# One PSUM group, one copy and one subtraction for the transposed weights of the first two query blocks

## The chip, the cores and the metric

The kernel runs on one core of a Trainium2 chip. The metric is the device time of one execution, in microseconds (us). The core has five engines with instruction streams of their own, which meet only in semaphores: TensorE (PE, with its weight loads shown as PEld), VectorE (DVE), ScalarE (ACT), GpSimd (POOL) and SyncE (SP).

## What is computed

The program is a whole transformer step for one sequence of 512 tokens and 1024 channels: a feed-forward layer, a mixer, a second feed-forward layer, and then a hybrid layer. The part that matters here is the attention of the hybrid layer, with 16 heads of 64 channels, in float32:

```python
def stick_breaking_attention(q, k, v):
    S = q.shape[2]
    outs = []
    for i in range(S // BLOCK_Q):
        q0, q1 = i * BLOCK_Q, (i + 1) * BLOCK_Q
        qb, kb, vb = q[:, :, q0:q1], k[:, :, :q1], v[:, :, :q1]
        z = jnp.einsum('bhqd,bhkd->bhqk', qb, kb).astype(jnp.float32) * SB_SCALE
        mask = jnp.arange(q1)[None, :] < jnp.arange(q0, q1)[:, None]
        log_1m_beta = jnp.where(mask, -jax.nn.softplus(z), 0.0)
        suffix = lax.cumsum(log_1m_beta, axis=3, reverse=True) - log_1m_beta
        w = jnp.where(mask, jnp.exp(jax.nn.log_sigmoid(z) + suffix), 0.0)
        outs.append(jnp.einsum('bhqk,bhkd->bhqd', w.astype(vb.dtype), vb))
    return jnp.concatenate(outs, axis=2)
```

Query block i (128 queries) sees the keys of blocks 0 to i, so its weights are a matrix of 128 by (i+1)*128. It has to be transposed, block by block, before it can be multiplied with the values.

## The kernel before

The attention works in 8 rounds (PAIRS), each for one pair of heads h = 0 and 1. Round 0 is written out, rounds 1 to 6 are one hardware loop, round 7 is written out again. Products are made from float32 split into a high and a low part, three matmuls for one (`three`, L2307 to L2309).

A round on TensorE is two weight slots of the large input projection (`in_slot`), 8 steps of 6 matmuls each, with 512 columns to a matmul. Between these steps stand the small pieces of the attention. Where each stands is written by hand in three tables, one for each engine: ATT_PE, ATT_ACT and ATT_DVE. A key from 0 to 15 is the step of the round, and its list is what runs ahead of that step's matmuls. So each engine's order is fixed, and only semaphores join them. The pieces are:

- ("Q", h, i): the scores of query block i, three matmuls on TensorE (L2754 to L2756); ScalarE makes two sigmoids of them (L1204, L1205), VectorE a scan and a product (L2076, L2080), which leaves the weights in the tile Wt and counts w_done.
- ("T", h, i): the transposes of query block i. TensorE turns i+1 blocks of 128 columns into PSUM bank 6 (L2772) and counts t_mm. ScalarE copies them to wTh, the high part (L1224), and counts thi_done. VectorE subtracts that copy from the bank into wTl, the low part (L2100), and counts tlo_done. All groups share bank 6, so a group on TensorE waits until the subtraction of the group ahead of it is done (`tlo_done`, L2770). The first of a round waits for the values' low part instead (`vlo_done`).
- ("PV", h): the weights by the values, eight matmuls (L2781, L2782). It needs all four groups of its head.
- ("hi", n, half) and ("lo", n, half): high and low part of half a weight slot (L1255 on ScalarE, L2132 on VectorE).
- ("k low",), ("q low",), ("q own",), ("k other",), ("sum", 0), ("V",), ("v2",): keys, queries, sums and values for this round and the next.

I write T(h,i) for the group of head h and query block i. The eight groups stand at steps 4, 5, 7, 8 for h = 0 and at steps 10, 12, 13, 15 for h = 1. Behind T(1,1) on TensorE come the six matmuls of step 12, then T(1,2). The wait of a group reads:

```python
pe.wait_ge(w_done, r * 8 + (idx + 1))
if idx == 0:
    pe.wait_ge(vlo_done, r + 1)
else:
    pe.wait_ge(tlo_done, r * 8 + idx)
for b in range(i + 1):
    last = nc.tensor.transpose(ps[:, 6, b * P:(b + 1) * P], wt_of(i)[:, b * P:(b + 1) * P], ident[:])
last.then_inc(t_mm, 1)
```

Of the kernel before, what the change touches and what calls it, by code (L numbers as in the profile page):

```python
# [16 lines left out]
fp32 = mybir.dt.float32  # L17
f32r = mybir.dt.float32r
bf16 = mybir.dt.bfloat16
ALU = mybir.AluOpType  # L20
ACT = mybir.ActivationFunctionType
AX = mybir.AxisListType

P = 128
T = 512
# [72 lines left out]
for n, (_, _, during) in enumerate(MIXER):  # L98
    for k in sorted(during):
        for step in during[k]:  # L100
            if n >= 2 and step[0] in ("S", "cols", "vt", "mm", "hy"):
                at = 8 * n + k + 3 if n > 3 else 8 * n + min(k + 1, 7)
# [12 lines left out]
MIX_READ = {entry[:2]: n + 1 for n, entry in enumerate(MIXER)}  # L115


ATT_PE = {0: [("Q", 0, 0), ("Q", 0, 1), ("PV", 1), ("V",)], 1: [("Q", 0, 2)], 2: [("Q", 0, 3)], 4: [("T", 0, 0), ("Q", 1, 0)],
          5: [("T", 0, 1)], 7: [("Q", 1, 1), ("T", 0, 2), ("Q", 1, 2)], 8: [("T", 0, 3)], 9: [("Q", 1, 3)],
          10: [("PV", 0), ("T", 1, 0)], 12: [("T", 1, 1)], 13: [("T", 1, 2)], 15: [("T", 1, 3)]}  # L120
ATT_ACT = {0: [("v2",), ("Q", 0, 0), ("sum", 1), ("Q", 0, 1), ("hi", 0, 0), ("V",)], 1: [("Q", 0, 2)], 2: [("Q", 0, 3), ("gah",)],
# [3 lines left out]
ATT_DVE = {0: [("Q", 0, 0), ("sum", 1), ("gate",), ("Q", 0, 1), ("lo", 0, 0), ("V",)], 1: [("Q", 0, 2)],  # L125
# [3 lines left out]
ATT_LATE = ("PV", 1), ("sum", 1), ("gate",), ("gah",), ("gal",)  # L129

# [24 lines left out]
def program(nc, a, out):  # L155
    with ExitStack() as ctx:
# [21 lines left out]
        ident = sb("ident", [P, P])  # L178
# [251 lines left out]

        def wt_of(i):
            return Wt[:, i * (i + 1) // 2 * P:(i + 1) * (i + 2) // 2 * P]

        HALF = slice(0, DK), slice(DK, 2 * DK)

# [340 lines left out]
        def _(act):  # L776
# [420 lines left out]
            def att_step(step, r):  # L1197
                kind, h = step[0], step[1] if len(step) > 1 else 0
                if kind == "Q":
                    i = step[2]  # L1200
                    idx, n = 4 * h + i, (i + 1) * P
                    act.wait_ge(q_mm, r * 8 + (idx + 1))
                    act.wait_ge(w_done, r * 8 + max(idx - 1, 0))
                    nc.scalar.activation(g1[:, idx % 2, 0:n], ps[:, 4 + idx % 2, 0:n], ACT.Sigmoid, scale=-1.0)  # L1204
                    nc.scalar.activation(be[:, idx % 2, 0:n], ps[:, 4 + idx % 2, 0:n], ACT.Sigmoid).then_inc(sig_done, 1)  # L1205
                elif kind == "V":
                    act.wait_ge(v_mm, r + 1)
                    act.wait_ge(pv_mm, r * 2)
                    bank = ps[:, 6, :].rearrange("p (b d) -> p b d", d=P)
                    for e in range(2):  # L1210
                        last = nc.scalar.activation(vph[:, e, :, HALF[e]], bank[:, :, HALF[e]], ACT.Copy)
                    last.then_inc(vhi_done, 1)
                    for e in range(2):
                        last = nc.scalar.activation(vp[:, e, :, HALF[e]], bank[:, :, HALF[e]], ACT.Copy)
                    last.then_inc(vp_done, 1)
                elif kind == "sum":
                    act.wait_ge(pv_mm, r * 2 + 1 if h == 0 else r * 2)
                    nc.scalar.activation(pvl[HALF[h], :], ps[HALF[1 - h], 7, :], ACT.Copy).then_inc(pv_low, 1)
                elif kind == "T":
                    i = step[2]  # L1220
                    idx = 4 * h + i
                    act.wait_ge(t_mm, r * 8 + (idx + 1))
                    act.wait_ge(pv_mm, r * 2 + h)
                    nc.scalar.activation(wTh[:, 0:i + 1, i * P:(i + 1) * P],  # L1224
                                         ps[:, 6, 0:(i + 1) * P].rearrange("p (b t) -> p b t", t=P), ACT.Copy).then_inc(thi_done, 1)
                elif kind == "gah":
                    act.wait_ge(ga_done, r)
                    nc.scalar.activation(gah[:, r - 1:r, :] if isinstance(r, int) else gah[:, bass.ds(act.snap(r - 1), 1), :],
                                         ga[:].unsqueeze(1), ACT.Copy).then_inc(gah_done, 1)
                elif kind == "hi":  # L1230
                    if isinstance(r, int) and r == PAIRS - 1:
                        hi_half(S_POOL + h + 1, step[2])
                    else:
                        hi_half(S_ATT + h + 3, step[2], r)
                elif kind == "v2":
                    act.wait_ge(slot_used, r * 2 + (S_ATT + 2))
                    nc.scalar.activation(v2[:], ps[:, 2, :], ACT.Copy).then_inc(ve_done, 1)
                elif kind == "sz":
                    act.wait_ge(slot_used, r * 2 + (S_ATT + 2))
                    act.wait_ge(zs_done, r)  # L1240
                    nc.scalar.activation(sz[:], ps[:, 3, :], ACT.Sigmoid).then_inc(sz_done, 1)
                elif kind == "k own":
                    read_k(r + 1)
                elif kind == "q own":
                    read_q(r + 1)
                elif kind == "k other":
                    read_k_other(r + 1)
# [163 lines left out]
        def _(dve):  # L1411
# [656 lines left out]
            def att_step(step, r):  # L2068
                kind, h = step[0], step[1] if len(step) > 1 else 0
                if kind == "Q":  # L2070

                    i = step[2]
# [22 lines left out]
                elif kind == "T":  # L2095
                    i = step[2]
                    idx = 4 * h + i
                    dve.wait_ge(thi_done, r * 8 + (idx + 1))
                    place = (slice(None), slice(0, i + 1), slice(i * P, (i + 1) * P))
                    nc.vector.tensor_tensor(wTl[place], ps[:, 6, 0:(i + 1) * P].rearrange("p (b t) -> p b t", t=P),  # L2100
                                            wTh[place].bitcast(fp32), ALU.subtract).then_inc(tlo_done, 1)
                elif kind == "gate":
                    dve.wait_ge(pv_sum, r * 2)
                    dve.wait_ge(zs_done, r)
# [199 lines left out]
        def _(pe):  # L2304
# [438 lines left out]
            def att_step(step, r):  # L2743
# [19 lines left out]
                elif kind == "T":  # L2763
                    i = step[2]
                    idx = 4 * h + i
                    pe.wait_ge(w_done, r * 8 + (idx + 1))
                    if idx == 0:
                        pe.wait_ge(vlo_done, r + 1)
                    else:
                        pe.wait_ge(tlo_done, r * 8 + idx)  # L2770
                    for b in range(i + 1):
                        last = nc.tensor.transpose(ps[:, 6, b * P:(b + 1) * P], wt_of(i)[:, b * P:(b + 1) * P], ident[:])  # L2772
                    last.then_inc(t_mm, 1)
                elif kind == "PV":

                    pe.wait_ge(tlo_done, r * 8 + 4 if h == 0 else r * 8)
# [176 lines left out]
```

## Time and profile before

| | before |
|---|---|
| median of 3 runs | 1530.57 us (1530.33 to 1530.58) |
| the profiled execution | 1530.44 us |
| span of its trace | 1528.8 us |
| TensorE busy | 1514.4 us (99%), 8932 matmuls |
| VectorE busy | 1014.7 us (66%) |
| ScalarE busy | 714.4 us (47%) |
| mean granted TensorE clock | 0.999 of full speed |

Durations come from the profiled execution. A row of the trace gives a start and a duration. TensorE's matmuls overlap: one of 512 columns is shown for 0.39 us, but the next one starts 0.23 us after it. So what a piece costs TensorE is read from the distance of the starts, and its duration only tells when its result is there. The start of a weight load (PEld) shows when a waiting matmul was let go, since the load comes first.

### The profile page before, as it was taken

To read this page: it belongs to the slowest core of one execution; us is meant where nothing else is said; L and a number is where in the kernel's file an instruction comes from. 1 tells how busy PE (TensorE), PEld (TensorE's weight loads), DVE (VectorE), ACT (ScalarE), POOL (GpSimd) and SP (SyncE) were. 2 spreads that over 40 slices of the span, in tenths; PEclk is the share of its full clock that TensorE was granted. 3 is DMA by queue.
4 is the path that set the end of the run, shared out by engine and by line. 5 is a ranking of instruction groups with operands and counts; after the bars stand their busy time and mean duration, and the time that the engine had idled before them with its cause. 6 is when DMAs were issued, how large, how long until landed. Compare 5 with 4: busy or idle time off the path is not lost.

```text
span 1528.8 us, 23058 instructions
## 1 busy us (share of the span) xinstructions
PE 1514.4 (99%) x8932; PEld 1334.6 (87%) x8932; DVE 1014.7 (66%) x1206; ACT 714.4 (47%) x1045; POOL 54.1 (4%) x101
## 2 busy tenths in 40 slices
PE   8999999999999999999999999999999999999998
PEld 7999998889888889899998888788888888888887
DVE  5888884237766838888885766688888775423243
ACT  6545543236566337545443224566666633312134
POOL 1000000002100002000000001000000000000001
PEclk9999999999999999999999999999999999999999
DMA  5233323322331231333326752222222222332321
GB/s 196 83 111 110 97 70 136 110 82 84 99 98 56 83 111 56 111 111 99 97 80 233 247 179 61 68 66 55 82 71 66 71 95 83 110 111 82 110 83 55
DMA packets 134909, 153.23 MB, mean 100 GB/s; under 512 B 3600, under 2 KB 123532, under 8 KB 134844
## 3 DMA queue, kind: packets, MB, share of 16 engines
q1 hardware_dynamic: 131584, 137.38, 28.5%
q0 software_dynamic: 3024, 14.88, 2.9%
q8 instruction: 46, 0.75, 0.2%
q14 instruction: 19, 0.16, 0.0%
q10 hardware_dynamic: 236, 0.06, 0.0%
HBM read 150.08 MB, written 2.23 MB: 100 GB/s over the span
## 4 chain that ended last, share of the span: by engine, by line
PE 96%; DVE 2%; ACT 1%; issue 0%; DMA 0%; DVEq 0%; ACTq 0%
PE ps L2307 21%; PE ps L2309 21%; PE ps L2308 21%; PE ps L2506 16%; PE ps L2511 8%; PE ps L2772 1%; PE ps L2670 1%; PE ps L2782 1%; PE ps L2755 1%; PE ps L2781 1%; PE ps L2754 1%; PE ps L2388 0%; PE ps L2737 0%; PE ps L2448 0%; DVE wl L1417 0%
## 5 line engine op out<-in xcount | busy, mean ns | idle before, releaser
L2307 PE MATMUL ps<-ah,wh 128*128 128x512 f32 (+1 forms) x1344 | 515.5, 384 | 3.1 <-DVE al L1471 1.2
L2309 PE MATMUL ps<-ah,wl 128*128 128x512 f32 (+1 forms) x1344 | 503.8, 375 | 0.0
L2308 PE MATMUL ps<-al,wh 128*128 128x512 f32 (+1 forms) x1344 | 503.0, 374 | 0.0
L2307 PEld LDWEIGHTS ps<-ah,wh 128*128 128x128 f32 x1344 | 253.8, 189 | 48.8 <-issue 2.3
L2309 PEld LDWEIGHTS ps<-ah,wl 128*128 128x128 f32 x1344 | 252.9, 188 | 45.9
L2308 PEld LDWEIGHTS ps<-al,wh 128*128 128x128 f32 x1344 | 253.5, 189 | 41.1
L1417 DVE TENSOR_TENSOR wl<-raw,wh 128x2048 fp32r<-128x2048 f32 x52 | 119.1, 2291 | 164.7 <-ACT wh L790 164.5
L790 ACT ACTIVATE wh<-raw 128x2048 fp32r<-128x2048 f32 x53 | 101.3, 1911 | 196.9 <-PE ps L2309 193.2
L2506 PE MATMUL ps<-al,wh 128*128 128x256 f32 x576 | 141.3, 283 | 0.0
L2506 PE MATMUL ps<-ah,wh 128*128 128x256 f32 x576 | 141.3, 283 | 0.0
L2506 PEld LDWEIGHTS ps<-al,wh 128*128 128x128 f32 x576 | 110.6, 192 | 0.1
L2506 PEld LDWEIGHTS ps<-ah,wh 128*128 128x128 f32 x576 | 110.6, 192 | 0.1
L2506 PE MATMUL ps<-sh,wh 128*128 128x256 f32 x432 | 106.0, 283 | 0.0
L2506 PE MATMUL ps<-sl,wh 128*128 128x256 f32 x432 | 106.0, 283 | 0.0
L2253 DVE TENSOR_TENSOR wl<-raw,wh 128x2048 fp32r<-128x2048 f32 x16 | 36.7, 2292 | 91.8 <-ACT wh L1345 91.8
L1345 ACT ACTIVATE wh<-raw 128x2048 fp32r<-128x2048 f32 x16 | 30.7, 1917 | 127.3 <-PE ps L2309 127.3
L2506 PEld LDWEIGHTS ps<-sh,wh 128*128 128x128 f32 x432 | 82.9, 192 | 0.0
L2506 PEld LDWEIGHTS ps<-sl,wh 128*128 128x128 f32 x432 | 82.9, 192 | 0.0
L2511 PE MATMUL ps<-ah,wl 128*128 128x256 f32 x576 | 80.9, 283 | 0.0
L2511 PEld LDWEIGHTS ps<-ah,wl 128*128 128x128 f32 x576 | 74.3, 192 | 0.0
L1649 DVE TENSOR_TENSOR wl<-raw,wh 128x1024 fp32r<-128x1024 f32 x54 | 66.0, 1222 | 11.5 <-ACT wh L961 11.5
L981 ACT ACTIVATE hid<-gate 128x512 f32 (+1 forms) x36 | 22.8, 633 | 100.1 <-DVE gate L1702 100.1
(397 smaller groups left out, 2404.3 us busy)
## 6 DMA issues: line engine op xcount, KB each, us to landing
raw<-in_w_ffn_in SPq DMA_DIRECT2D x74, 512.0 KB, 3.6
raw<-in_w_ffn_out SPq DMA_DIRECT2D x22, 1024.0 KB, 5.0
raw<-in_w_in SPq DMA_DIRECT2D x36, 512.0 KB, 4.8
raw<-in_w_in SPq DMA_DIRECT2D x14, 1024.0 KB, 5.6
ada_raw<-in_w_ada POOLq DMA_DIRECT2D x8, 1536.0 KB, 7.3
raw<-in_w_mix_in SPq DMA_DIRECT2D x10, 1024.0 KB, 5.3
raw<-in_w_ffn_in SPq DMA_DIRECT2D x7, 1024.0 KB, 5.2
raw<-in_w_mix_out SPq DMA_DIRECT2D x4, 1024.0 KB, 4.9
```

The lines of the kernel that those rows point to most:

```text
L790: nc.scalar.activation(wh[n % 2][:], raw[n % 2][:], ACT.Copy).then_inc(hi_done, 2 if n + 1 in AHEAD else 1)
L981: nc.scalar.activation(hid[:, bass.ds(i * 4 + 2 * (PLAIN[f] + par), 2), COLS[h]], (gate1, gate2)[h][:], ACT.Silu).then_inc(gate_silu, 1)
L1345: nc.scalar.activation(wh[n % 2][:], raw[n % 2][:], ACT.Copy).then_inc(hi_done, 1)
L1417: nc.vector.tensor_tensor(wl[n % 2][:], raw[n % 2][:], wh[n % 2][:].bitcast(fp32), ALU.subtract).then_inc(lo_done, 2 if n + 1 in AHEAD else 1)
L1649: nc.vector.tensor_tensor(ring_of(wl, f, k), weight_of(f, PRODUCTS[k]), ring_of(wh, f, k).bitcast(fp32), ALU.subtract).then_inc(p_lo, 1)
L2253: nc.vector.tensor_tensor(wl[n % 2][:], raw[n % 2][:], wh[n % 2][:].bitcast(fp32), ALU.subtract).then_inc(lo_done, 1)
L2307: nc.tensor.matmul(bank, w[0], m[0], start=start, stop=False, skip_group_check=shared)
L2308: nc.tensor.matmul(bank, w[0], m[1], start=False, stop=False, skip_group_check=shared)
L2309: return nc.tensor.matmul(bank, w[1], m[0], start=False, stop=stop, skip_group_check=shared)
L2506: nc.tensor.matmul(ps[:, bank, COLS[nb]], ring_of(wh, f, k)[:, kk, nb * P:(nb + 1) * P], (high, low)[part][:, kk, :], start=name in OPENS ...
L2511: last = nc.tensor.matmul(ps[:, bank, COLS[nb]], ring_of(wl, f, k)[:, kk, nb * P:(nb + 1) * P], high[:, kk, :], start=False, stop=kk == KD ...
L2670: last = nc.tensor.matmul(ps[:, 6 + w, at:at + DV + 1], E[:, u % 2, b, t * P:(t + 1) * P], vS[:, h, b, :], start=j == 0, stop=j == len(see ...
```

## The change

T(h,0) and T(h,1) become one group, at the place of T(h,1). TensorE's entries ("T", h, 0) go out of the three tables. The entry ("T", h, 1) now makes three transposes in bank 6: block (query 0, key 0) in the first quarter, (query 1, key 0) in the second and (query 1, key 1) in the fourth. The third quarter keeps whatever was there. One ScalarE copy and one VectorE subtraction take the whole bank as 2 times 256 columns; what lands from the third quarter in wTh and wTl is never read, since the value matmuls of key block 1 start at query block 1. The counters step by 2 at once, so that all later counts stay as they were. The merged group waits for the values' low part with h = 0, and for the group ahead of it with h = 1.

```diff
-ATT_PE = {0: [("Q", 0, 0), ("Q", 0, 1), ("PV", 1), ("V",)], 1: [("Q", 0, 2)], 2: [("Q", 0, 3)], 4: [("T", 0, 0), ("Q", 1, 0)],
+ATT_PE = {0: [("Q", 0, 0), ("Q", 0, 1), ("PV", 1), ("V",)], 1: [("Q", 0, 2)], 2: [("Q", 0, 3)], 4: [("Q", 1, 0)],
...
-          10: [("PV", 0), ("T", 1, 0)], 12: [("T", 1, 1)], 13: [("T", 1, 2)], 15: [("T", 1, 3)]}
+          10: [("PV", 0)], 12: [("T", 1, 1)], 13: [("T", 1, 2)], 15: [("T", 1, 3)]}
...
+        def turned_blocks(i):
+
+            return [(0, 0, 0), (1, 0, 1), (1, 1, 3)] if i == 1 else [(i, b, b) for b in range(i + 1)]
+
+        def turned_place(i):
+
+            first, n = (0, 2 * P) if i == 1 else (i * P, P)
+            return (slice(None), slice(0, i + 1), slice(first, first + n)), ps[:, 6, 0:(i + 1) * n].rearrange("p (b t) -> p b t", t=n)
+
...
-                    nc.scalar.activation(wTh[:, 0:i + 1, i * P:(i + 1) * P],
-                                         ps[:, 6, 0:(i + 1) * P].rearrange("p (b t) -> p b t", t=P), ACT.Copy).then_inc(thi_done, 1)
+                    place, turned = turned_place(i)
+                    nc.scalar.activation(wTh[place], turned, ACT.Copy).then_inc(thi_done, 2 if i == 1 else 1)
...
-                    place = (slice(None), slice(0, i + 1), slice(i * P, (i + 1) * P))
-                    nc.vector.tensor_tensor(wTl[place], ps[:, 6, 0:(i + 1) * P].rearrange("p (b t) -> p b t", t=P),
-                                            wTh[place].bitcast(fp32), ALU.subtract).then_inc(tlo_done, 1)
+                    place, turned = turned_place(i)
+                    nc.vector.tensor_tensor(wTl[place], turned, wTh[place].bitcast(fp32), ALU.subtract).then_inc(tlo_done, 2 if i == 1 else 1)
...
-                    if idx == 0:
+                    if idx == 1:
                         pe.wait_ge(vlo_done, r + 1)
                     else:
-                        pe.wait_ge(tlo_done, r * 8 + idx)
-                    for b in range(i + 1):
-                        last = nc.tensor.transpose(ps[:, 6, b * P:(b + 1) * P], wt_of(i)[:, b * P:(b + 1) * P], ident[:])
-                    last.then_inc(t_mm, 1)
+                        pe.wait_ge(tlo_done, r * 8 + (idx if i > 1 else idx - 1))
+                    for q, b, at in turned_blocks(i):
+                        last = nc.tensor.transpose(ps[:, 6, at * P:(at + 1) * P], wt_of(q)[:, b * P:(b + 1) * P], ident[:])
+                    last.then_inc(t_mm, 2 if i == 1 else 1)
```

The first place: TensorE in the loop, from the last value matmul of PV(0) to the matmuls of step 10. Before:

```order
L2782 MATMUL ps<-wTl,vph 128x256
L2781 MATMUL ps<-wTh,vp 128x128
L2782 MATMUL ps<-wTl,vph 128x128
L2772 MATMUL ps<-ident,Wt 128x128 [waits tlo_done,w_done]
L2307 MATMUL ps<-ah,wh 128x512
L2308 MATMUL ps<-al,wh 128x512
```

and after:

```order
L2790 MATMUL ps<-wTl,vph 128x256
L2789 MATMUL ps<-wTh,vp 128x128
L2790 MATMUL ps<-wTl,vph 128x128
L2315 MATMUL ps<-ah,wh 128x512
L2316 MATMUL ps<-al,wh 128x512
```

The lone transpose of T(1,0) is gone from here, and the projection's matmul follows the value matmul at once.

The second place: TensorE in the loop, from T(1,1) over step 12 to T(1,2). Before:

```order
L2772 MATMUL ps<-ident,Wt 128x128 [waits tlo_done,w_done]
L2772 MATMUL ps<-ident,Wt 128x128
L2307 MATMUL ps<-ah,wh 128x512
L2308 MATMUL ps<-al,wh 128x512
L2309 MATMUL ps<-ah,wl 128x512
L2307 MATMUL ps<-ah,wh 128x512
L2308 MATMUL ps<-al,wh 128x512
L2309 MATMUL ps<-ah,wl 128x512
L2766 REGISTER_ALU
L2772 MATMUL ps<-ident,Wt 128x128 [waits tlo_done,w_done]
```

and after:

```order
L2780 MATMUL ps<-ident,Wt 128x128 [waits tlo_done,w_done]
L2780 MATMUL ps<-ident,Wt 128x128 x2
L2315 MATMUL ps<-ah,wh 128x512
L2316 MATMUL ps<-al,wh 128x512
L2317 MATMUL ps<-ah,wl 128x512
L2315 MATMUL ps<-ah,wh 128x512
L2316 MATMUL ps<-al,wh 128x512
L2317 MATMUL ps<-ah,wl 128x512
L2774 REGISTER_ALU
L2780 MATMUL ps<-ident,Wt 128x128 [waits tlo_done,w_done]
```

The group has one transpose more, and the same six matmuls stand between it and the next group.

The third place: ScalarE in the loop, from the first half of the weight slot's high part to the sum behind T(1,1). Before:

```order
L1255 ACTIVATE wh<-raw 128x1024 [waits slot_used]
L1223 REGISTER_ALU [waits t_mm]
L1224 ACTIVATE wTh<-ps 128x128 [waits pv_mm]
L1255 ACTIVATE wh<-raw 128x1024
L1224 ACTIVATE wTh<-ps 128x2x128 [waits pv_mm,t_mm]
L1267 ACTIVATE q<-ps 64x512 [waits q_mm]
L1267 ACTIVATE q<-ps 64x512
L1218 ACTIVATE acc<-ps 64x512 [waits pv_mm]
```

and after:

```order
L1264 ACTIVATE wh<-raw 128x1024 [waits slot_used]
L1264 ACTIVATE wh<-raw 128x1024
L1232 REGISTER_ALU [waits t_mm]
L1234 ACTIVATE wTh<-ps 128x2x256 [waits pv_mm]
L1276 ACTIVATE q<-ps 64x512 [waits q_mm]
L1276 ACTIVATE q<-ps 64x512
L1227 ACTIVATE acc<-ps 64x512 [waits pv_mm]
```

The copy is of 512 columns in place of 256, and the wait for TensorE (t_mm) has moved from the copy itself to a register instruction ahead of it. In rounds 0 and 7 the copy itself waits, before and after.

## Rows read from the trace of the kernel before

**Rows 1.** Page, head: busy time, share of the span, instructions.
```profile
span 1528.8 us, 23058 instructions
PE 1514.4 (99%) x8932; PEld 1334.6 (87%) x8932; DVE 1014.7 (66%) x1206; ACT 714.4 (47%) x1045; POOL 54.1 (4%) x101
PEclk9999999999999999999999999999999999999999
```

**Rows 2.** Waits, 960 to 1260 us: who waited for whom, total, times, longest.
```profile
ACT wTh L1224 <- PE ps L2772: 65.6, 50, 3.0
DVE wTl L2100 <- ACT wTh L1224: 35.9, 42, 1.6
...
PEld ps L2772 <- issue: 0.4, 1, 0.4
```

**Rows 3.** Lines by form, attention: group, count, busy us, mean ns, idle before.
```profile
L2772 PE MATMUL ps<-ident,Wt 128*128 128x128 f32 x160 | 28.2, 274 | 0.0
...
L2100 DVE TENSOR_TENSOR wTl<-ps,wTh 128x512 fp32r<-128x512 f32 x16 | 11.1, 692 | 8.9 <-ACT wTh L1224 8.9
L1224 ACT ACTIVATE wTh<-ps 128x512 fp32r<-128x512 f32 x16 | 9.6, 600 | 16.1 <-PE ps L2772 16.1
...
L2100 DVE TENSOR_TENSOR wTl<-ps,wTh 128x256 fp32r<-128x256 f32 x16 | 6.7, 421 | 9.5 <-ACT wTh L1224 9.5
L1224 ACT ACTIVATE wTh<-ps 128x256 fp32r<-128x256 f32 x16 | 6.2, 385 | 13.4 <-PE ps L2772 13.4
```

**Rows 4.** Timeline: start, duration, engine; TensorE at T(0,0) and Q(1,0), round 0.
```profile
985.57 0.27 PE L2772 MATMUL ps<-ident,Wt 128*128 128x128 f32 x1
985.59 0.30 PE L2754 MATMUL ps<-k,q 128*128 128x128 f32 x1
...
985.89 0.48 PE L2307 MATMUL ps<-ah,wh 128*128 128x512 f32 x1
```

**Rows 5.** Timeline, TensorE: Q(0,0) of the next round, with no transpose ahead.
```profile
1007.24 0.22 PE L2754 MATMUL ps<-k,q 128*128 128x128 f32 x1
...
1007.46 0.36 PE L2754 MATMUL ps<-k,q 128*128 128x256 f32 x1
```

**Rows 6.** Timeline, TensorE: the last of PV(0), and T(1,0).
```profile
997.72 0.28 PE L2782 MATMUL ps<-wTl,vph 128*128 128x128 f32 x1
...
997.83 0.30 PE L2772 MATMUL ps<-ident,Wt 128*128 128x128 f32 x1
...
998.20 0.39 PE L2308 MATMUL ps<-al,wh 128*128 128x512 f32 x1
```

**Rows 7.** Timeline, round 0: T(1,1), its copy, its subtraction, T(1,2).
```profile
1000.72 0.39 PE L2772 MATMUL ps<-ident,Wt 128*128 128x128 f32 x2
...
1000.86 0.48 PE L2307 MATMUL ps<-ah,wh 128*128 128x512 f32 x1
...
1001.14 0.39 ACT L1224 ACTIVATE wTh<-ps 128x256 fp32r<-128x256 f32 x1 [1.28 <-PE ps L2772]
...
1001.56 0.42 DVE L2100 TENSOR_TENSOR wTl<-ps,wTh 128x256 fp32r<-128x256 f32 x1 [1.19 <-ACT wTh L1224]
...
1002.10 0.48 PEld L2772 LDWEIGHTS ps<-ident,Wt 128*128 128x128 f32 x3
1002.33 0.49 PE L2772 MATMUL ps<-ident,Wt 128*128 128x128 f32 x3
...
1002.57 0.48 PE L2307 MATMUL ps<-ah,wh 128*128 128x512 f32 x1
```

**Rows 8.** Timeline, VectorE at T(1,2), and TensorE's load for T(1,3).
```profile
1003.90 0.54 DVE L2100 TENSOR_TENSOR wTl<-ps,wTh 128x384 fp32r<-128x384 f32 x1
...
1005.19 0.58 PEld L2772 LDWEIGHTS ps<-ident,Wt 128*128 128x128 f32 x4
```

**Rows 9.** Timeline: a late load let go by VectorE, ahead of attention.
```profile
960.19 0.75 DVE L1471 SCALAR_TENSOR_TENSOR al<-tt,mod,ah 128x512 fp32r<-128x512 f32 x1
...
960.99 0.19 PEld L2307 LDWEIGHTS ps<-ah,wh 128*128 128x128 f32 x1 [0.23 <-DVE al L1471]
961.02 0.47 PE L2307 MATMUL ps<-ah,wh 128*128 128x512 f32 x1
```

**Rows 10.** Timeline, round 7: a late load of a transpose group, T(0,3).
```profile
1207.21 0.42 PEld L2772 LDWEIGHTS ps<-ident,Wt 128*128 128x128 f32 x4 [0.37 <-issue]
1207.24 0.63 PE L2772 MATMUL ps<-ident,Wt 128*128 128x128 f32 x4
```

**Rows 11.** Timeline, feed-forward: ScalarE let go by TensorE, twice.
```profile
99.24 1.12 PE L2511 MATMUL ps<-ah,wl 128*128 128x256 f32 x8
...
100.48 1.06 ACT L961 ACTIVATE wh<-sq 128x1024 fp32r<-128x1024 f32 x1 [1.21 <-PE ps L2511]
...
102.12 1.12 PE L2511 MATMUL ps<-ah,wl 128*128 128x256 f32 x8
...
103.28 0.60 ACT L977 ACTIVATE up<-ps 128x512 f32<-128x512 f32 x1 [0.79 <-PE ps L2511]
```

8 rows, old and new, of tables (ATT_ACT, ATT_DVE) are left out of this document.

## The prediction

> **What bounds the kernel now.** I read the head of the page first. TensorE is busy for 99% of the span at a clock granted at its full level, 2.4 GHz, all along, while VectorE stands at 66% and ScalarE at 47% [rows 1]. So only two things can move the time: the distance from one TensorE start to the next, and a wait that TensorE does not have today. The waits of the attention come next. ScalarE waits for the transposes (65.6 us in 50 waits) and VectorE for the copies (35.9 us in 42), but of TensorE's own transpose groups one alone is late, by 0.4 us in all [rows 2]. The time that ScalarE and VectorE save is thus worth nothing by itself. What counts is the transposes' places in TensorE's queue, and how long the chain of transposes, copy and subtraction is, because the next group waits for its end (one bank for all). I looked for the spot where that chain is tightest, which is between T(1,1) and T(1,2).
>
> **What ScalarE and VectorE save.** The merged copy is 600 ns, the merged subtraction 692 ns; the two-block ones are 385 and 421 ns [rows 3]. One copy and one subtraction in each head go. Nobody on TensorE waits for either engine here, so I cost this at nothing. The cover is TensorE's own work; were it gone, this would be a gain of some tenths of a us in a round.
>
> A rule speaks for the change here: the Trainium skill, VectorE: DVE Perf Modes, section "The TRN2 errata", says that each instruction pays a fixed latency and advises tiles of 512 elements or more. Twice the columns take 1.56 times as long on ScalarE (600 over 385) and 1.64 times on VectorE, so the trace agrees. It makes a throughput gain on engines that have time to spare, and adds nothing to the sum.
>
> **TensorE's queue, head 0.** T(0,0) and Q(1,0) together take 985.89 - 985.57 = 0.32 us from start to start [rows 4]. Q without a transpose ahead of it takes 1007.46 - 1007.24 = 0.22 us [rows 5]. So 0.10 us goes at step 4. The merged group has three transposes for two. Two take 1000.86 - 1000.72 = 0.14 us of the queue and three take 1002.57 - 1002.33 = 0.24 us [rows 7], so 0.10 us comes back at step 5. The sum is nothing.
>
> **TensorE's queue, head 1.** From the last value matmul over T(1,0) to the second matmul of step 10 it is 998.20 - 997.72 = 0.48 us [rows 6]. Without the transpose it should be 0.11 us (the distance from the value matmul to its successor, in the same rows) and 0.23 us for a matmul of 512 columns, 0.34 us in all. The trace has no value matmul followed by a projection matmul, so this is bounded: from 0.48 (nothing goes) to 0.34, and I take 0.34, since both matmuls are of the same kind. That is -0.14, and the third transpose at T(1,1) is +0.10: -0.04 us in a round, and 0.3 us in 8 rounds.
>
> **The chain behind T(0,1).** T(0,2) is two steps away, past ten other matmuls or more, and VectorE has the first subtraction of the round less ahead of it. The chain grows by 0.6 us (worked out next) against over 1 us of room, so I expect no wait there.
>
> **The chain behind T(1,1).** Here only six matmuls stand between. In round 0 the group starts at 1000.72, the copy at 1001.14, the subtraction at 1001.56 and ends at 1001.98; TensorE's load for T(1,2) is at 1002.10 [rows 7]. From the end of a VectorE instruction to the load that it releases takes 960.99 - 960.94 = 0.05 us [rows 9]. So the room today is 0.12 - 0.05 = 0.07 us. The change lengthens the chain in three places: the group ends 0.10 us later (the spans of three and two transposes, 0.49 and 0.39 [rows 7]), the copy takes 0.215 us more and the subtraction 0.271 us more [rows 3]. That is 0.59 us. TensorE itself comes 0.10 us later. The load is therefore late by 0.59 - 0.10 - 0.07 = 0.42 us.
>
> TensorE doesn't lose all of that, since a load normally starts ahead of its matmul: 1002.33 - 1002.10 = 0.23 us [rows 7]. A late one starts 0.03 us ahead [rows 9, 10]. So 0.20 us of the lateness is absorbed, and 0.22 us is lost. A group with a late load then takes a little longer in the queue, some 0.02 us by an estimate from the spans, 0.63 against 0.60 for four transposes. I take **0.24 us** for a round.
>
> **The register wait.** In the loop the copy's wait for TensorE now stands on a register instruction ahead of it, and ScalarE has nothing else to do by then. The trace has such a case: ScalarE starts L961 at 100.48, 0.12 us after TensorE's end (99.24 + 1.12); L977, which waits itself, starts 0.04 us after the end at 103.24 [rows 11]. So the chain is 0.08 us longer in the six rounds of the loop. Before, this register wait belonged to T(1,0)'s copy, which ScalarE reached long after the transpose was done. The bounds are 0 and 0.08 us; I take 0.08, since the two forms in the rows are those of the order. A loop round then loses 0.32 us.
>
> **Behind that wait.** Queued behind T(1,2) on TensorE are all later matmuls of the round, and every one shifts. Who is late next? T(1,3) waits for T(1,2)'s subtraction, which ends at 1004.44 with the load at 1005.19 [rows 8]: 0.75 us of room. VectorE comes to it up to 0.6 us later, TensorE 0.3 us later, so about 0.4 us of room stays. The last subtraction of the round follows T(1,3) with both engines idle ahead of it, so PV(1) keeps its distance. The half slots of `hi` and `lo` run earlier than before, since T(0,0) and T(1,0) no longer stand ahead of them on ScalarE and VectorE.
>
> **The sum.** Rounds 0 and 7: 2 x (0.24 - 0.04) = 0.40 us. Rounds 1 to 6: 6 x (0.32 - 0.04) = 1.68 us. Together +2.1 us. The profiled execution took 1530.44 us, 0.13 us under the median; on the median of 1530.57 that is **1532.7 us**, 0.14% slower, within what a measurement of this kernel can hardly tell from no change (0.2%, or 3.1 us).
>
> The Trainium skill states this very effect: Perfetto Trace Analysis, section "Optimizing Scalar/DVE Operations", says that where these engines aren't saturated but cause bubbles on others, breaking instructions up may let work complete sooner. The change is the reverse of that. By this rule the chain decides, as in my sum; by the rule on fixed latency nothing would be lost, which is the first rival. That TensorE's load for T(1,2) comes only 0.12 us after the subtraction's end today [rows 7] agrees with the rule of breaking up; a wait there is shown by no row of before.
>
> **Rivals.**
>
> *No wait appears.* If the load is let go earlier than I work out, only the queue's gain stays: 8 x -0.04 = -0.3 us, 1530.3 us. The point from which it decides is a chain 0.42 us shorter in rounds 0 and 7. Against it: each term is the length of a shape that the trace has 16 times. 12%.
>
> *The wait, and the lone transposes free nothing.* The matmul behind a transpose group has a distance of about 0.32 us to its successor instead of 0.23, and so has the one behind a Q piece. If TensorE pays that after PV(0) too, and Q(1,0) alone still takes 0.32 us, then the 0.10 and 0.14 us do not go. That is 0.24 us a round, 1.9 us in all: 1532.7 + 1.9 = 1534.6 us, slower by 0.27%. It decides from 0.12 us a round on. For it: no row has a value matmul ahead of a projection matmul. Against it: rows 5 have the Q piece alone at 0.22 us. 18%, with what a wait at T(1,3) could add.
>
> *Faster.* For over 3.1 us a round would have to gain 0.4 us, where the two removed groups hold 0.24 us in all. It needs a cost of a group that the starts don't show. 3%.
>
> *The change doesn't do what it says.* The order of the instructions shows one copy and one subtraction in place of two on each engine, and 160 transposes as before, so I give this no chance of its own.
>
> **How the numbers follow.** The forecast has 67%, the rivals 12, 18 and 3%. In its own range the register wait may be worth nothing (-0.5 us), and the wait may be 0.1 us longer or shorter in each round (0.8 us either way): 1531.4 to 1533.5 us. The range for 8 in 10 takes in the upper bound of the queue's term at PV(0) (+1.1 us: 1533.8) and reaches some way to both neighbours: 1530.9 to 1534.2 us. Slower by over 0.2% (from 1533.63 us on) has 19%, faster by over 0.2% 3%, and within it 78%.
>
> **What would show it.** In the changed kernel's waits, TensorE's load for the transposes has 8 waits on the VectorE subtraction. Counted from the end of the load ahead (0.04 us ahead of the normal start), they are of about 0.46 us in rounds 0 and 7 and 0.54 us in the loop. T(1,1)'s copy starts 0.53 us after its group in rounds 0 and 7 and about 0.61 us after it in the loop. Step 10's first matmul follows PV(0) by 0.11 us and its successor follows it by 0.23 us. Q(1,0) takes 0.22 us. Were there no wait at T(1,2), or one at T(0,2), T(1,3) or PV too, the prediction would be wrong in its mechanism; were the distances around the removed groups unchanged, in its size.

## The result, and the profile after

| | before | changed |
|---|---|---|
| median | 1530.57 us (9 runs, 1530.33 to 1530.78) | 1534.60 us (9 runs, 1534.44 to 1534.83) |
| span of the trace | 1528.8 us | 1532.8 us |

The change makes the kernel slower by 4.0 us, a ratio of 1.0026 (95% interval 1.0017 to 1.0036). The forecast was 1532.7 us with 1534.2 as the upper end. The sign and the place were right. The size was not: half of the loss was missing.

The head of the changed kernel's page answers to [rows 1]. The busy times differ by 1 us at most, and 16 instructions are gone on VectorE and on ScalarE, two for each round:

```profile
span 1532.8 us, 23016 instructions
PE 1515.4 (99%) x8932; PEld 1334.4 (87%) x8932; DVE 1015.5 (66%) x1190; ACT 714.1 (47%) x1029; POOL 54.1 (4%) x101
```

Busy times don't show where 4 us went. The waits do. Here are those of the changed kernel from 960 to 1260 us (who waited for whom, total, times, longest), beside [rows 2]:

```profile
PEld ps L2780 <- issue: 6.0, 9, 0.7
...
PE ps L2780 <- DVE wTl L2109: 2.4, 8, 0.3
```

One late load of a transpose group has become nine. Eight of them are new, and TensorE itself sat idle in all eight for the VectorE subtraction. Before, it did not once.

This is T(1,1) to T(1,2) in round 0 of the changed kernel, in order of time, beside [rows 7]:

```profile
1000.61 0.49 PE L2780 MATMUL ps<-ident,Wt 128*128 128x128 f32 x3
...
1000.86 0.47 PE L2315 MATMUL ps<-ah,wh 128*128 128x512 f32 x1
...
1001.19 0.60 ACT L1234 ACTIVATE wTh<-ps 128x512 fp32r<-128x512 f32 x1 [1.65 <-issue]
...
1001.89 0.69 DVE L2109 TENSOR_TENSOR wTl<-ps,wTh 128x512 fp32r<-128x512 f32 x1 [2.04 <-ACT wTh L1234]
...
1002.10 0.40 PE L2317 MATMUL ps<-ah,wl 128*128 128x512 f32 x1
...
1002.70 0.31 PEld L2780 LDWEIGHTS ps<-ident,Wt 128*128 128x128 f32 x3 [0.64 <-issue]
1002.73 0.52 PE L2780 MATMUL ps<-ident,Wt 128*128 128x128 f32 x3 [0.24 <-DVE wTl L2109]
...
1003.00 0.48 PE L2315 MATMUL ps<-ah,wh 128*128 128x512 f32 x1
```

T(1,2) starts 0.63 us after the matmul ahead of it, where the normal distance is 0.23 us. That is 0.40 us lost. The group then takes 1003.00 - 1002.73 = 0.27 us of the queue, 0.02 to 0.03 us more than one that isn't late. In the loop the copy comes later still. This is round 1:

```profile
1031.72 0.49 PE L2780 MATMUL ps<-ident,Wt 128*128 128x128 f32 x3
1032.38 0.60 ACT L1234 ACTIVATE wTh<-ps 128x512 fp32r<-128x512 f32 x1 [1.74 <-PE ps L2780]
...
1033.08 0.69 DVE L2109 TENSOR_TENSOR wTl<-ps,wTh 128x512 fp32r<-128x512 f32 x1 [1.83 <-ACT wTh L1234]
1033.20 0.40 PE L2317 MATMUL ps<-ah,wl 128*128 128x512 f32 x1
...
1033.89 0.31 PEld L2780 LDWEIGHTS ps<-ident,Wt 128*128 128x128 f32 x3 [0.73 <-issue]
1033.92 0.52 PE L2780 MATMUL ps<-ident,Wt 128*128 128x128 f32 x3 [0.32 <-DVE wTl L2109]
```

The distance is 0.72 us here, so 0.49 us are lost. The copy starts 0.66 us after its group, against 1001.19 - 1000.61 = 0.58 us in round 0. This 0.08 us is what the prediction gave the wait on the register instruction.

The queue behind PV(0), beside [rows 6]:

```profile
997.69 0.27 PE L2790 MATMUL ps<-wTl,vph 128*128 128x128 f32 x1
997.80 0.44 PE L2315 MATMUL ps<-ah,wh 128*128 128x512 f32 x1
998.08 0.39 PE L2316 MATMUL ps<-al,wh 128*128 128x512 f32 x1
```

From the last value matmul to the second matmul of step 10 it is 0.39 us, between the 0.34 of the forecast and the 0.48 of before.

The whole loss then adds up from the trace. A round of the kind of 0 and 7 loses 0.40 (late start) + 0.02 (longer group) + 0.01 (queue: -0.09 at T(1,0), +0.10 for the third transpose) = 0.43 us, a round of the loop 0.52 us. 2 x 0.43 + 6 x 0.52 = 4.0 us, which is the difference of the spans.

### The profile page after: what moved, and what is told of

It is laid out like the page before. It is cut to its first block, busy times and chain, and to the rows that moved or that the text cites. A ratio compares the mean times of both kernels' runs of the same rounds, so it can differ in the third digit from the quotient of the medians.

```text
span 1532.8 us, 23016 instructions
## 1 busy us (share of the span) xinstructions
PE 1515.4 (99%) x8932; PEld 1334.4 (87%) x8932; DVE 1015.5 (66%) x1190; ACT 714.1 (47%) x1029; POOL 54.1 (4%) x101
## 4 chain that ended last, share of the span: by engine, by line
PE 95%; DVE 2%; ACT 1%; issue 1%; DMA 0%; DVEq 0%; ACTq 0%
PE ps L2315 21%; PE ps L2317 21%; PE ps L2316 21%; PE ps L2514 16%; PE ps L2519 8%; PE ps L2780 1%; PE ps L2678 1%; PE ps L2790 1%; PE ps L2763 1%; PE ps L2789 1%; PE ps L2762 1%; PE ps L2396 0%; PE ps L2745 0%; DVE wTl L2109 0%; PE ps L2456 0%
```

## Experiments

Each run was timed in several rounds against the kernel before on the same chip, whose median lay between 1530.45 and 1530.55 us.

### Which head, and is it the room

The first question is whether the wait at T(1,2) is all of the loss. Two kernels make the change at one head alone. Their edit is in the condition of the merged group, and in the tables, where the entries of the other head come back:

```diff
-            return [(0, 0, 0), (1, 0, 1), (1, 1, 3)] if i == 1 else [(i, b, b) for b in range(i + 1)]
+            return [(0, 0, 0), (1, 0, 1), (1, 1, 3)] if (h, i) == (0, 1) else [(i, b, b) for b in range(i + 1)]
```

**Head 0 alone (h0).**

> The change at head 0 alone: T(0,0) and T(0,1) merged, T(1,0) and T(1,1) as before. By my steps T(0,2) has over 1 us of room, no wait appears, and TensorE's queue comes out even (0.11 us less at Q(1,0), 0.10 us more at T(0,1)): 1530.4 to 1530.7 us. If a merged group costs something that is not the wait, the time shows half of the whole loss, 1532.4 us.

Measured: 1530.84 us against 1530.55 (ratio 1.0002, 0.9992 to 1.0011). This is T(0,1) to T(0,2) in round 0:

```profile
987.50 0.49 PE L2780 MATMUL ps<-ident,Wt 128*128 128x128 f32 x3
988.08 0.60 ACT L1234 ACTIVATE wTh<-ps 128x512 fp32r<-128x512 f32 x1 [1.37 <-issue]
988.78 0.69 DVE L2109 TENSOR_TENSOR wTl<-ps,wTh 128x512 fp32r<-128x512 f32 x1 [1.28 <-ACT wTh L1234]
990.83 0.32 PEld L2780 LDWEIGHTS ps<-ident,Wt 128*128 128x128 f32 x3
```

The subtraction ends at 989.47, 1.36 us ahead of the load. The same longer chain stands here, and costs nothing that the interval can tell from zero. The time is still 0.1 us above the expected range: a round of the loop takes 30.65 us against 30.61 before. No wait at T(0,2) goes with it, and where these 0.04 us a round come from is open.

**Head 1 alone (h1).**

> The change at head 1 alone: T(1,0) and T(1,1) merged, T(0,0) and T(0,1) as before. The wait at T(1,2) is all of the loss: 8 waits of 0.40 to 0.49 us at the start of T(1,2) against the normal distance, 0.02 us of a longer group and 0.01 us in the queue, 1534.4 us. If the loss is shared by both heads, 1532.4 us.

Measured: 1534.58 us (1.0027, 1.0016 to 1.0037). In its waits TensorE sits idle for the subtraction 8 times, 2.4 us in all, as in the changed kernel. All of the loss is at head 1.

**T(1,1) one step earlier (earlier).**

```diff
-          10: [("PV", 0)], 12: [("T", 1, 1)], 13: [("T", 1, 2)], 15: [("T", 1, 3)]}
+          10: [("PV", 0)], 11: [("T", 1, 1)], 13: [("T", 1, 2)], 15: [("T", 1, 3)]}
```

> The changed kernel with T(1,1) one step earlier in TensorE's table (step 11 in place of 12), so that twelve matmuls stand between it and T(1,2) in place of six. ScalarE's and VectorE's orders, shapes, steps of two and wait orders stay. The room grows by six matmuls, 1.4 us, against a wait of some 0.7 us: no wait at T(1,2), and what stays is the queue alone, +0.01 us a round by the trace of the changed kernel: 1530.4 to 1530.8 us. T(1,1) stands one step behind PV(0) now, and ScalarE finishes its half slot 0.4 us ahead of it. If merging costs anything beside the wait, the time stays above 1531 us.

Measured: 1530.70 us (1.0001, 0.9991 to 1.0011). With twelve matmuls in between, the load of T(1,2) comes when TensorE gets to it:

```profile
999.35 0.49 PE L2780 MATMUL ps<-ident,Wt 128*128 128x128 f32 x3
999.93 0.60 ACT L1234 ACTIVATE wTh<-ps 128x512 fp32r<-128x512 f32 x1 [0.28 <-issue]
1000.63 0.69 DVE L2109 TENSOR_TENSOR wTl<-ps,wTh 128x512 fp32r<-128x512 f32 x1 [0.67 <-ACT wTh L1234]
1002.21 0.48 PEld L2780 LDWEIGHTS ps<-ident,Wt 128*128 128x128 f32 x3
1002.44 0.49 PE L2780 MATMUL ps<-ident,Wt 128*128 128x128 f32 x3
```

The copy is 0.58 us and the subtraction 1.28 us behind the group, as in the changed kernel: the chain is as slow as it was, and one table entry makes 3.9 us of it vanish. So the loss is the room at that one spot.

### How much of it is the length of the chain

**The kernel before with a wide copy at T(1,1) (wide).** On ScalarE:

```diff
-                    nc.scalar.activation(wTh[:, 0:i + 1, i * P:(i + 1) * P],
-                                         ps[:, 6, 0:(i + 1) * P].rearrange("p (b t) -> p b t", t=P), ACT.Copy).then_inc(thi_done, 1)
+                    n = 4 if (h, i) == (1, 1) else i + 1
+                    nc.scalar.activation(wTh[:, 0:n, i * P:(i + 1) * P],
+                                         ps[:, 6, 0:n * P].rearrange("p (b t) -> p b t", t=P), ACT.Copy).then_inc(thi_done, 1)
```

and the same n in VectorE's subtraction.

> The kernel before, all eight groups of a round as they were, but at T(1,1) the copy and the subtraction take the whole bank (512 columns) in place of 256; the other two quarters land where nobody reads. Nothing else differs: no merged group, no step of two, the register wait stays at T(1,0)'s copy. It measures the length of the chain alone. By my working the chain is 0.215 + 0.271 = 0.49 us longer against 0.07 us of room, late by 0.42 us; 0.20 us of that is absorbed by the load's lead, and 0.24 us a round is lost: 8 x 0.24 = +1.9 us, 1532.5 us. If the lead absorbs nothing, 8 x 0.42 = +3.4 us, 1534.0 us. If the chain's length is not what costs, 1530.6 us.

Measured: 1532.79 us against 1530.46 (1.0016, 1.0006 to 1.0025), +2.3 us, 0.4 us more than expected.

```profile
1000.72 0.38 PE L2774 MATMUL ps<-ident,Wt 128*128 128x128 f32 x2
1001.14 0.60 ACT L1225 ACTIVATE wTh<-ps 128x512 fp32r<-128x512 f32 x1 [1.28 <-PE ps L2774]
...
1001.77 0.69 DVE L2102 TENSOR_TENSOR wTl<-ps,wTh 128x512 fp32r<-128x512 f32 x1 [1.41 <-ACT wTh L1225]
...
1002.58 0.31 PEld L2774 LDWEIGHTS ps<-ident,Wt 128*128 128x128 f32 x3 [0.52 <-issue]
1002.61 0.52 PE L2774 MATMUL ps<-ident,Wt 128*128 128x128 f32 x3
```

Group to copy is 0.42 us and copy to subtraction 0.63 us, just as worked out. But the load comes at 1002.58 and the subtraction ends at 1002.46: 0.12 us, where the prediction had 0.05 from [rows 9]. Before, the load stood 0.12 us behind the subtraction's end as well [rows 7], so there was no room. The load is late by 1002.58 - 1002.10 = 0.48 us, 0.20 of that is absorbed, and with 0.02 to 0.03 us of a longer group some 0.30 us a round is lost, 2.4 us in 8 rounds against the 2.3 us measured. That the load's lead absorbs 0.20 us holds.

### Where the other half came from

By a hand-over I mean the time from one engine's instruction to the one that it releases on another engine. In the changed kernel all three are slower than I had worked out: transposes to copy 0.58 us in place of 0.53, copy to subtraction 0.70 in place of 0.64, subtraction to load 0.12 in place of 0.05. Together that is 0.18 us. Two things could be behind it that I had not looked at: the semaphores step by two, and a matmul has two waits. The runs below test them. What they have in common is put together behind the last of them.

**Steps of one (inc1).**

```diff
-                    nc.scalar.activation(wTh[place], turned, ACT.Copy).then_inc(thi_done, 2 if i == 1 else 1)
+                    nc.scalar.activation(wTh[place], turned, ACT.Copy).then_inc(thi_done, 1)
```

and so for t_mm and tlo_done, with 6 counts a round in all waits, as `r * 6 + (3 * h + i)`.

> The changed kernel, but every semaphore of the transposes counts by one at a time (six counts a round, where the changed kernel steps by two for a merged group). Shapes, places and waits stay. In the changed kernel each of the three hand-overs at T(1,1) is slower than I had it: transposes to copy 0.09 us from the group's modelled end in place of 0.03-0.04, copy to subtraction 0.70 us from start to start in place of 0.64, subtraction's end to the load 0.12 us in place of 0.05. Theory A, a step of two is handed over some 0.06 us later than a step of one: the copy starts 0.53 us after the group (round 0), the subtraction 0.64 us after the copy, the load 0.05 us after the subtraction's end; T(1,2)'s wait is 0.18 us shorter and the time 8 x 0.18 = 1.4 us shorter, 1533.2 us. Theory B, the 2 x 256 shape of the tile or the bank itself makes the hand-overs slow: nothing changes, 1534.6 us.

Measured: 1533.20 us against 1530.46 (1.0018, 1.0009 to 1.0028). Round 0:

```profile
1000.74 0.49 PE L2780 MATMUL ps<-ident,Wt 128*128 128x128 f32 x3
1001.27 0.60 ACT L1234 ACTIVATE wTh<-ps 128x512 fp32r<-128x512 f32 x1 [1.60 <-PE ps L2780]
...
1001.90 0.69 DVE L2109 TENSOR_TENSOR wTl<-ps,wTh 128x512 fp32r<-128x512 f32 x1 [1.93 <-ACT wTh L1234]
...
1002.71 0.31 PEld L2780 LDWEIGHTS ps<-ident,Wt 128*128 128x128 f32 x3 [0.52 <-issue]
```

The time is the one that theory A gave, but not by its steps, so the hit is partly luck. The copy starts 0.53 and the subtraction 0.63 us on: these two hand-overs were the step of two, 0.05 and 0.07 us. Whether it is the step of the engine that releases or of the one that waits, this run doesn't say, since both have changed. The third hand-over was not the step. The load still comes 0.12 us after the subtraction's end (1002.59). In the loop it comes after 0.05 us, and there the order of the instructions differs: counts of six gave the wait for the weights a register instruction of its own, and left the late wait alone on the matmul. This is round 1:

```profile
1032.94 0.69 DVE L2109 TENSOR_TENSOR wTl<-ps,wTh 128x512 fp32r<-128x512 f32 x1 [1.70 <-ACT wTh L1234]
...
1033.68 0.32 PEld L2780 LDWEIGHTS ps<-ident,Wt 128*128 128x128 f32 x3 [0.54 <-DVE wTl L2109]
...
1033.68 0.55 PE L2780 MATMUL ps<-ident,Wt 128*128 128x128 f32 x3
```

So [rows 9] were a matmul with one wait, and T(1,2) has two. That is the 0.07 us of the third hand-over. TensorE doesn't win all of it: the first transpose starts with its load, at 1033.68, and the group takes 0.31 us of the queue in place of 0.27.

**Steps of two in the kernel before (inc2).** All counts of the three semaphores are doubled; the shapes stay.

```diff
-                    nc.vector.tensor_tensor(wTl[place], ps[:, 6, 0:(i + 1) * P].rearrange("p (b t) -> p b t", t=P),
-                                            wTh[place].bitcast(fp32), ALU.subtract).then_inc(tlo_done, 1)
+                    nc.vector.tensor_tensor(wTl[place], ps[:, 6, 0:(i + 1) * P].rearrange("p (b t) -> p b t", t=P),
+                                            wTh[place].bitcast(fp32), ALU.subtract).then_inc(tlo_done, 2)
```

> The kernel before with all counts of the transposes' three semaphores doubled: each group, copy and subtraction steps by two, and all waits ask for twice the number. Shapes and places as before. Theory A (a step of two is handed over 0.06 us later): T(1,1)'s copy starts 0.47 us after the group in place of 0.42, the subtraction 0.47-0.48 us after the copy in place of 0.42, the load of T(1,2) comes 0.12 us after the subtraction's end at the earliest; the chain is 0.18 us longer against 0.07 us of room, and the load's lead of 0.20 us absorbs the 0.11 us, so the time hardly moves: 1530.6 to 1531.0 us. Theory B (the shape): all hand-overs as before, 1530.6 us.

Measured: 1530.83 us against 1530.46 (1.0002, 0.9993 to 1.0012).

```profile
1000.89 0.38 PE L2772 MATMUL ps<-ident,Wt 128*128 128x128 f32 x2
1001.36 0.39 ACT L1224 ACTIVATE wTh<-ps 128x256 fp32r<-128x256 f32 x1 [1.33 <-issue]
...
1001.85 0.42 DVE L2100 TENSOR_TENSOR wTl<-ps,wTh 128x256 fp32r<-128x256 f32 x1 [1.24 <-ACT wTh L1224]
...
1002.39 0.36 PEld L2772 LDWEIGHTS ps<-ident,Wt 128*128 128x128 f32 x3 [0.16 <-issue]
1002.50 0.49 PE L2772 MATMUL ps<-ident,Wt 128*128 128x128 f32 x3
```

With the shapes of before, the copy comes 0.47 us after the group and the subtraction 0.49 us after the copy, where both were 0.42 [rows 7]. So the shape 2 x 256 is not the cause, and the step of two is. The load is 0.12 us after the subtraction's end (1002.27), the same as with a step of one in inc1's round 0, so VectorE's step adds nothing there. Nor does it in the loop:

```profile
1032.50 0.42 DVE L2100 TENSOR_TENSOR wTl<-ps,wTh 128x256 fp32r<-128x256 f32 x1 [1.24 <-ACT wTh L1224]
...
1032.98 0.42 PEld L2772 LDWEIGHTS ps<-ident,Wt 128*128 128x128 f32 x3
```

The load is 0.06 us after the end (1032.92), against 0.05 us in inc1's loop with a step of one. In both the wait for the subtraction stands alone on the matmul. A releaser that steps by two is thus no slower here. In round 0 the load is late but T(1,2) starts on time, 0.11 us behind it: the lead absorbs small latenesses whole.

**TensorE's two waits exchanged (pewait).**

```diff
-                    pe.wait_ge(w_done, r * 8 + (idx + 1))
                     if idx == 1:
                         pe.wait_ge(vlo_done, r + 1)
                     else:
                         pe.wait_ge(tlo_done, r * 8 + (idx if i > 1 else idx - 1))
+                    pe.wait_ge(w_done, r * 8 + (idx + 1))
```

> The changed kernel with TensorE's two waits ahead of each transpose group in the other order (first the subtraction of the group ahead, then the weights, which are there long before). In the changed kernel the load of T(1,2) comes 0.12 us after the subtraction's end, with a step of two; in the run with steps of one it was 0.12 us in round 0, where the matmul carries both waits, and 0.05 us in the loop, where it carries the late one alone. Theory A, of two waits on one matmul the late one costs 0.07 us more when it is written last: in rounds 0 and 7 the load comes 0.05 us after the subtraction's end and T(1,2) starts some 0.07 us earlier. In the loop the late wait now falls on a register instruction; if that costs TensorE what it costs ScalarE (0.05 to 0.08 us), nothing is won there and the time is 1534.3 us; if it costs nothing, 1533.9 us. Theory B, the order of the waits does nothing: 0.12 us everywhere, 1534.4 us.

Measured: 1534.76 us (1.0028, 1.0017 to 1.0038). Round 0:

```profile
1001.94 0.69 DVE L2109 TENSOR_TENSOR wTl<-ps,wTh 128x512 fp32r<-128x512 f32 x1 [2.04 <-ACT wTh L1234]
...
1002.68 0.31 PEld L2780 LDWEIGHTS ps<-ident,Wt 128*128 128x128 f32 x3 [0.58 <-DVE wTl L2109]
1002.69 0.55 PE L2780 MATMUL ps<-ident,Wt 128*128 128x128 f32 x3
```

The load comes 0.05 us after the subtraction's end (1002.63), and only now does the profile name VectorE as what released it, where it had "issue" at 0.12. So with two waits on a matmul the order in which they are written matters for the load. In the loop, where the late wait moved to a register instruction, it was 0.13 us, and nothing was won. My total was still too low: the time is 0.5 us above the expected one and no better than the changed kernel's, and T(1,2) takes 0.30 us of the queue in place of 0.27. That the matmul loses part of what the load wins, I can see. In the loop the distances ahead of and behind T(1,2) come to 0.70 + 0.30 = 1.00 us against 0.72 + 0.27 = 0.99 in the changed kernel, but a whole round takes 31.20 us against 31.13. So most of what is lost there stands elsewhere in the round, and I have not traced it.

**ScalarE's two waits exchanged (swap).**

```diff
-                    act.wait_ge(t_mm, r * 8 + (idx + 1))
                     act.wait_ge(pv_mm, r * 2 + h)
+                    act.wait_ge(t_mm, r * 8 + (idx + 1))
```

> The changed kernel with ScalarE's two waits ahead of the copies in the other order, so that in the loop the wait for the value matmuls (long done) stands on the register instruction or none does, and the wait for the transposes on the copy itself. If a wait on a register instruction costs 0.08 us where the engine has nothing else to do: T(1,1)'s copy starts 0.58 us after the group in the loop as in round 0 (now 0.66), T(1,2) starts 0.63 us after the matmul ahead in the loop as in round 0 (now 0.72), and the time is 6 x 0.08 = 0.5 us shorter, 1534.1 us. If the 0.08 us has another cause in the loop, 1534.6 us.

Measured: 1534.32 us against 1530.46 (1.0025, 1.0015 to 1.0035), 0.3 us less than the changed kernel's 1534.60 where 0.5 was expected. Round 1:

```profile
1031.81 0.49 PE L2780 MATMUL ps<-ident,Wt 128*128 128x128 f32 x3
1032.42 0.60 ACT L1234 ACTIVATE wTh<-ps 128x512 fp32r<-128x512 f32 x1 [1.69 <-PE ps L2780]
```

The copy starts 0.61 us after the group, down from 0.66 in the loop, but in round 0 it is up from 0.58 to 0.62 us. So of the 0.08 us that the loop had over round 0, 0.05 went with the wait off the register instruction. The other 0.03 us is the price of writing the late wait last. It fits: 6 x 0.05 - 2 x 0.04 = 0.2 us.

**What these runs have in common.** The kept traces also record the instructions that only wait, which the views leave out. They show on which instruction the late wait of each hand-over stood. A semaphore instruction is one that does nothing but wait:

| hand-over | late wait on the instruction itself | on a semaphore instruction ahead of it | on a register instruction ahead of it |
|---|---|---|---|
| group of three to copy | 0.53 us (inc1, round 0) | 0.58 us (changed kernel, round 0), 0.61 to 0.62 us (swap) | 0.61 us (inc1, loop), 0.66 us (changed kernel, loop, with a semaphore instruction behind the register instruction) |
| copy to subtraction, 512 columns | 0.63 us (inc1, wide) | 0.70 us (changed kernel, swap) | none |
| subtraction's end to load | 0.05 to 0.06 us (inc1 and inc2 in the loop, pewait in round 0) | 0.12 us (before, changed kernel, wide) | 0.12 to 0.13 us (pewait, loop) |

In all eleven traces no ScalarE or VectorE instruction of work that steps a semaphore by two has a wait of its own, and none on these engines or TensorE has two waits: the wait that is left over stands on a semaphore or register instruction ahead of it. That is what the step of two and the order of the waits have in common.

It also tells whose step of two it is. In the changed kernel's round 0 the semaphore instruction ahead of the subtraction starts 0.03 us after the copy's end, just as inc1's subtraction itself does, and the subtraction starts 0.07 us behind it. In the loop ScalarE's register instruction that waits for the group starts 0.53 us after it, with TensorE's step of two in the changed kernel as with its step of one in inc1. So it is the copy's and the subtraction's own step of two that makes them late, and not the step of the engine that they wait for.

Two readings from before have to be set right. The section on the change says that in rounds 0 and 7 the copy itself waits, before and after. In the changed kernel its waits stand on a semaphore instruction ahead of it. And T(1,2)'s late wait stood on such an instruction already before the change; the order of the instructions shows both waits at the matmul.

### Is there a version that beats both

**All put right (best).** T(1,1) at step 11, steps of one, ScalarE's late wait on the copy.

> The changed kernel with all that the runs have shown put right: T(1,1) one step earlier on TensorE, steps of one in the transposes' counts, and ScalarE's late wait on the copy itself. With T(1,1) earlier no engine that sets the end waits, so the two other edits have nothing left to win: same as with T(1,1) earlier alone, 1530.5 to 1530.9 us, which is not faster than the kernel before (1530.5). If merging saves TensorE anything, it shows here, as 1530.2 us or less.

Measured in 5 rounds: 1530.67 us against 1530.45 (1.0001, 0.9992 to 1.0010). No version is faster than the kernel before. There is nothing to win: a merged group saves 0.09 to 0.11 us of TensorE's queue and its third transpose costs 0.10 us.

## Why the prediction was right or wrong, point by point

- **TensorE bounds, and what the other two engines save is worth nothing.** Right: with the wait gone (earlier, best) 16 fewer instructions on each gave nothing.
- **Head 0 comes out even.** Right in both terms: Q(1,0) takes 0.21 us in the changed kernel, the merged group 0.24. No wait at T(0,2); h0, 0.3 us above the kernel before but within its interval, shows none either.
- **Head 1's queue, -0.04 us.** The step that took 0.34 us behind PV(0) was 0.05 us too low: 0.39 us. The net is +0.01 us, so 0.05 us a round above the forecast and 0.4 us in all rounds. It lay inside the bounds of 0.34 and 0.48.
- **A wait at T(1,2), and nowhere else.** Right: 8 waits, one in a round. T(1,3) and PV(1) showed none.
- **The size of that wait.** Wrong, and this is the term that was mis-sized: 0.40 and 0.49 us of late start were measured, 0.22 and 0.30 us were worked out. The shapes were right (0.60 and 0.69 us), and so was the absorbed 0.20 us (wide). The step that failed was that hand-overs between engines cost what the rows of before show, where the late wait stands on the waiting instruction itself. The change makes two of them slower: 0.05 us at the copy and 0.06 to 0.07 us at the subtraction, which now step by two themselves and have their waits on an instruction ahead (inc1, inc2 and the traces' waiting instructions). The third was 0.07 us slower than I had it before the change already, because T(1,2) has two waits and the late one stands ahead of the matmul (wide, inc1's loop, pewait). 0.18 us in 8 rounds is 1.4 us. I had priced the third from [rows 9], a matmul with one wait, though the order of the instructions showed two at T(1,2). [rows 7] could not show the mistake: there, 0.12 us between the subtraction's end and the load was read as 0.07 us of room and 0.05 us of hand-over. There was no room at all.
- **The register wait, 0.08 us in the loop.** Right in size: 0.66 against 0.58 us, and 0.61 against 0.53 us in inc1, where in round 0 the wait stands on the copy itself.
- **The rival that gave 1534.6 us** hit the time by another mechanism. It had TensorE save nothing at the two removed groups; it does save there, 0.09 and 0.11 us.
- **The two rules of the Trainium skill.** Fixed latency (VectorE: DVE Perf Modes, "The TRN2 errata") held for the durations (600 ns for 512 columns, 385 for 256 on ScalarE) and moved no time. The advice of 512 elements is given there for sources in SBUF; the copy and the subtraction read from PSUM, for which the section's table has a fixed term too. What "Optimizing Scalar/DVE Operations" of Perfetto Trace Analysis says of smaller instructions on a chain that another engine waits for was right: wide alone, 256 columns more in two instructions, cost 2.3 us.

The missing 1.9 us are thus 1.4 us of hand-overs, 0.4 us of queue, and 0.1 us that rows read to 0.01 us and taken 8 times can't place.

## What to carry to other kernels

When pieces are merged on engines that have time to spare, the instructions saved there win nothing by themselves, and the time rises where the engine that bounds the kernel waits for the merged piece's end. Look for the spot with the least room between two uses of the shared buffer, and move the piece ahead by one step before it is made longer. When room is counted in hundredths of a us, read the price of a hand-over from a row whose waiting instruction carries the same waits and steps its own semaphore by the same number. Look for the instruction that the late wait really stands on: here it cost 0.05 to 0.08 us more when it stood on one ahead. And treat a load that follows its releaser by 0.12 us as one that may already be waiting.

## What the runs showed of the hardware that I had not expected

- An instruction of ScalarE or VectorE that steps a semaphore by two has no wait of its own in any of the eleven traces; its wait stands on a semaphore instruction ahead of it. It starts 0.05 us later than one with a step of one on ScalarE (0.47 against 0.42 us, 0.58 against 0.53) and 0.06 to 0.07 us later on VectorE (0.49 against 0.42, 0.70 against 0.63). The step of the engine that releases shows no such price: from VectorE to TensorE it is 0.12 us both ways in round 0, and 0.06 against 0.05 us in the loop.
- Where two waits stand ahead of one matmul in the program, its load starts 0.12 us after the releaser's end if the late one is written last, and 0.05 us if it is written first or stands alone. The traces show the wait written last on a semaphore instruction ahead of the load. The profile then says "issue" for the one and names the engine for the other. On ScalarE the order is worth 0.04 us at a step of two (swap, round 0: 0.62 against 0.58 us) and 0.06 us at a step of one (best against inc1, round 0: 0.59 against 0.53 us).
- A load's lead of 0.23 us shrinks to 0.03 us or less before TensorE loses anything, and T(1,2) started on time with a lead of 0.11 us (inc2).
